# Gate products of a Griffin recurrent block: four float32 matmuls replaced by twelve float32r ones per pair of blocks, and moved half a weight tile to a tile and a half later

## The reference, cut to what matters

```python
u = jnp.einsum('bsd,de->bse', h, w_in) + b_in          # 1024 -> 2048
x_br = u[..., :D_RNN]
y_br = jax.nn.gelu(u[..., D_RNN:], approximate=True)
xp = jnp.pad(x_br, ((0, 0), (CONV_WIDTH - 1, 0), (0, 0)))
xc = conv_b + xp[:, 0:S] * conv_w[0]
for tap in range(1, CONV_WIDTH):
    xc = xc + xp[:, tap:tap + S] * conv_w[tap]
xb = xc.reshape(B, S, N_RG_BLOCKS, RG_BLOCK)             # 8 blocks of 128
r = jax.nn.sigmoid(jnp.einsum('bsnc,nce->bsne', xb, w_ga) + b_ga).reshape(B, S, D_RNN)
ig = jax.nn.sigmoid(jnp.einsum('bsnc,nce->bsne', xb, w_gx) + b_gx).reshape(B, S, D_RNN)
log_a = -RG_C * r * jax.nn.softplus(-a_param)
a = jnp.exp(log_a)
mult = jnp.sqrt(-jnp.expm1(2.0 * log_a))
b_seq = mult * (ig * xc)
# hs[t] = a[t] * hs[t-1] + b_seq[t]
out = hs * y_br
return jnp.einsum('bse,ed->bsd', out, w_o) + b_o
```

## Time and profile before

| what | value |
|---|---|
| median of 3 runs | 977.24 us (976.72 to 977.33) |
| span of the profiled execution | 975.9 us |
| what the runs have around that span | 1.3 us |
| PE busy | 968.3 us, 99% of the span |
| DVE, ACT, POOL busy | 70%, 60%, 7% |
| granted TensorE clock | full in all 40 slices |
| recurrent stage (`rin` 0 to `rout` 3) on PE | about 313.4 to 398.4 us |
| gate products (L589) | 16 matmuls in 32 records, 324.6 to 348 us |

### The profile page before, as it was taken

How to read it: one execution, slowest core, us unless ns; L and a number is a source line. 1 busy time by engine, 2 the same in 40 slices (tenths; PEclk the granted TensorE clock), 3 DMA queues, 4 the chain that set the end, 5 groups by cost and what they waited for, 6 DMA issues and landing times.

```text
span 975.9 us, 13399 instructions
## 1 busy us (share of the span) xinstructions
PE 968.3 (99%) x5146; PEld 826.0 (85%) x5146; DVE 680.5 (70%) x1161; ACT 588.6 (60%) x1042; POOL 66.2 (7%) x80
## 2 busy tenths in 40 slices
PE   8999999999999999999999999999999999999997
PEld 6887788888888898888888888888888888988886
DVE  5877786666568789666665588778767554877564
ACT  6777755454457897645454467547876555684443
POOL 1322110000000242000000000000011000000000
PEclk9999999999999999999999999999999999999999
DMA  9753545655455445555655556445543544335551
GB/s 368 296 194 134 184 173 186 224 176 211 174 196 185 146 165 192 182 187 184 226 178 207 177 198 250 173 175 188 198 165 105 193 148 170 132 133 209 177 189 44
DMA packets 27119, 180.33 MB, mean 185 GB/s; under 512 B 2992, under 2 KB 3888, under 8 KB 6320
## 3 DMA queue, kind: packets, MB, share of 16 engines
q1 hardware_dynamic: 26336, 176.98, 50.7%
q0 software_dynamic: 288, 2.10, 0.6%
q10 hardware_dynamic: 432, 0.39, 0.1%
HBM read 178.41 MB, written 1.05 MB: 184 GB/s over the span
## 4 chain that ended last, share of the span: by engine, by line
PE 99%; DMA 1%; DVE 0%; ACT 0%; SPq 0%; issue 0%; DVEq 0%
PE bank L338 25%; PE bank L293 16%; PE bank L295 16%; PE bank L294 16%; PE bank L346 13%; PE bank L308 1%; PE bank L468 1%; PE bank L484 1%; PE bank L589 1%; PE bank L518 1%; PE bank L309 1%; DMA front<-in_front 1%; PE bank L529 1%; PE bank L404 0%; PE bank L399 0%; PE bank L400 0%
## 5 line engine op out<-in xcount | busy, mean ns | idle before, releaser
L1349 DVE TENSOR_TENSOR lo<-raw,hi 128x1024 fp32r<-128x1024 f32 x318 | 375.9, 1229 | 20.1 <-ACT hi L822 19.9
L822 ACT ACTIVATE hi<-raw 128x1024 fp32r<-128x1024 f32 x318 | 320.3, 1050 | 100.1 <-PE bank L295 98.2
L338 PE MATMUL bank<-X,hi 128*128 128x512 f32 x1016 | 266.3, 394 | 0.0
L338 PEld LDWEIGHTS bank<-X,hi 128*128 128x128 f32 x1016 | 185.0, 189 | 32.8
L346 PEld LDWEIGHTS bank<-X,lo 128*128 128x128 f32 x1016 | 138.5, 190 | 10.1
L346 PE MATMUL bank<-X,lo 128*128 128x256 f32 x1016 | 141.6, 282 | 0.0
L853 ACT ACTIVATE bt<-bank 128x256 f32<-128x256 f32 x135 | 51.0, 380 | 141.5 <-PE bank L338 133.1
L1363 DVE TENSOR_TENSOR zr<-bank,bt 128x256 f32<-128x256 f32 x64 | 27.2, 424 | 108.9 <-ACT bt L853 108.9
L293 PE MATMUL bank<-hi,zh 128*128 128x512 f32 x256 | 100.0, 390 | 0.0
L295 PE MATMUL bank<-hi,zl 128*128 128x512 f32 x256 | 99.8, 390 | 0.0
L294 PE MATMUL bank<-lo,zh 128*128 128x512 f32 x256 | 99.6, 389 | 0.0
(11 more groups left out here) (345 smaller groups left out, 1420.5 us busy)
## 6 DMA issues: line engine op xcount, KB each, us to landing
raw<-in_w SPq DMA_DIRECT2D x64, 1024.0 KB, 4.7
raw<-in_rin SPq DMA_DIRECT2D x8, 1024.0 KB, 4.8
raw<-in_wk SPq DMA_DIRECT2D x4, 1024.0 KB, 10.3
raw<-in_wq SPq DMA_DIRECT2D x4, 1024.0 KB, 8.3
raw<-in_wo SPq DMA_DIRECT2D x4, 1024.0 KB, 4.7
raw<-in_mk SPq DMA_DIRECT2D x4, 1024.0 KB, 4.8
raw<-in_mv SPq DMA_DIRECT2D x4, 1024.0 KB, 4.8
raw<-in_rout SPq DMA_DIRECT2D x4, 1024.0 KB, 4.6
```

The costliest lines, as they stand in the source:

```text
L338: return PE.matmul(bank[b][:, :], wh[:, c:c + P], x[:, k_, :, :].rearrange("p a b -> p (a b)"), start=k_ == 0, stop=k_ == NC - 1, skip_gro ...
L822: ACTE.activation(hi[u_ % HIS][:, c], raw[u_ % RAW][:, c], ACT.Copy).then_inc(hi_cut, 1)
L1349: DVE.tensor_tensor(lo[u_ % RAW][:, c], raw[u_ % RAW][:, c], hi[u_ % HIS][:, c].bitcast(F32), ALU.subtract).then_inc(lo_cut, 1)
```

## The change

The gate weights `gw` and the convolution output `xc` are now split into float32r parts. ACT rounds `gw` into `gwh` and DVE subtracts to `gwl`, in two pieces each of 128x1024, inside the first MLP (steps 8 and 10). ACT rounds `xc` two blocks at a time into `xch` (`xc_highs`, 128x512), and DVE makes `xcl` (`xc_lows`). `xch` and `xcl` have room for four blocks. `gates(n)` on PE is now two `mm3`, six matmuls. The places move: blocks 0 and 1 stand in the middle of tile 2, blocks 2 and 3 in the middle of tile 3, blocks 4 and 5 in the first half of tile 4 and blocks 6 and 7 in the first half of tile 5 (each after its sixth of eight steps). On ACT every pair of gates is read one `to_x` later, and `xc_highs(i)` closes each step. The loads and their queues stay; POOL's load of `gw` goes to another slot.

```diff
-    gw = slot("gw", 14, [2, NC, P])
+    gw = slot("gw", 8, [2, NC, P])
+    gwh, gwl = slot("gwh", 14, [2, NC, P], F32R), slot("gwl", 4, [2, NC, P], F32R)
+    xch, xcl = slot("xch", 11, [4, S], F32R), slot("xcl", 11, [4, S], F32R, off=4096)
...
-                    if j == 1 and k_ == 4:
+                    if j == 0 and k_ == 6:
                         for n in within:
                             gates(n)
...
         def gates(n):
-            p.wait_ge(xc_made, n + 1)
-            p.wait_ge(gatew_in, 16)
+            p.wait_ge(xc_low, n // 2 + 1)
+            p.wait_ge(gw_low, 2)
             for m, b in ((0, 6 * (1 - n % 2)), (1, 7 - 6 * (n % 2))):
                 done = fill(("gate", n, m), b)
-                PE.matmul(bank[b][:, 0:S], gw[:, m, n, :], xc[:, n, :], start=True, stop=True).then_inc(done, 1)
+                mm3(bank[b][:, 0:S], gwh[:, m, n, :], gwl[:, m, n, :], xch[:, n % 4, :], xcl[:, n % 4, :], True, True).then_inc(done, 1)
...
         for i in range(1, 4):
-            cols("rin", i, X2, (2, 3) if i % 2 else (4, 5))
-            gates(2 * i - 2)
-            gates(2 * i - 1)
-        plain("rin", 4, X, (4, 5), (6, 7))
-        for i in range(5, 8):
+            half("rin", i, 0, X2, (4, 2)[i % 2])
+            if i > 1:
+                gates(2 * i - 4)
+                gates(2 * i - 3)
+            half("rin", i, 1, X2, (5, 3)[i % 2])
+        plain("rin", 4, X, (4, 5), (4, 5))
+        plain("rin", 5, X, (2, 3), (6, 7))
+        for i in range(6, 8):
             plain("rin", i, X, (2, 3) if i % 2 else (4, 5))
...
# ACT, in the first MLP; DVE has the matching subtraction into gwl
+                if n == 0 and i in (8, 10):
+                    m_ = i // 2 - 4
+                    a.wait_ge(gatew_in, 16)
+                    ACTE.activation(gwh[:, m_, :, :], gw[:, m_, :, :], ACT.Copy).then_inc(gw_high, 1)
...
# ACT
+        def xc_highs(i):
+            n = 2 * i
+            a.wait_ge(xc_made, n + 2)
+            if i >= 2:
+                a.wait_ge(*full["gate", n - 3, 1])
+                a.wait_ge(xc_low, i - 1)
+            ACTE.activation(xch[:, n % 4:n % 4 + 2, :], xc[:, n:n + 2, :], ACT.Copy).then_inc(xc_high, 1)
...
         for i in range(4):
             to_x(i)
-            if i:
-                gates(2 * i - 2)
-                gates(2 * i - 1)
+            if i > 1:
+                gates(2 * i - 4)
+                gates(2 * i - 3)
+            xc_highs(i)
         at_tile("rin", 4)
-        gates(6)
-        gates(7)
+        gates(4)
+        gates(5)
...
         to_y(4, ACT.Identity)
+        gates(6)
+        gates(7)
...
# DVE
+        def xc_lows(i):
+            n = 2 * i
+            d.wait_ge(xc_high, i + 1)
+            DVE.tensor_tensor(xcl[:, n % 4:n % 4 + 2, :], xc[:, n:n + 2, :], xch[:, n % 4:n % 4 + 2, :].bitcast(F32),
+                              ALU.subtract).then_inc(xc_low, 1)
...
         def to_x(i):
             lo_to(2 * (T_OF["rin", i] + 2))
+            if i:
+                xc_lows(i - 1)
...
         for i in range(4):
             to_x(i)
+        lo_to(2 * (T_OF["rin", 4] + 2) + 1)
+        xc_lows(3)
         lo_to(2 * (T_OF["rin", 4] + HIS))
```

More of the change, by code:

```diff
@@ L118, in build @@
     tap_made, xc_made, t_made = sem("tap_made"), sem("xc_made"), sem("t_made")
+    gw_high, gw_low, xc_high, xc_low = sem("gw_high"), sem("gw_low"), sem("xc_high"), sem("xc_low")
     gi_made, a_made, aa_made, mass_made, root_made, drive_made = (
@@ L1530, in mlp @@
                     at_tile(f"w2_{n}", i - 1)
+                if n == 0 and i in (8, 10):
+                    m_ = i // 2 - 4
+                    d.wait_ge(gw_high, m_ + 1)
+                    DVE.tensor_tensor(gwl[:, m_, :, :], gw[:, m_, :, :], gwh[:, m_, :, :].bitcast(F32), ALU.subtract).then_inc(gw_low, 1)
         mlp(0, 0, "wo")
```

## The result

The changed kernel takes 981.18 us (median of 5 runs, 980.51 to 981.95) against 977.33 us for the kernel before (976.72 to 977.85): a ratio of 1.0041, 95% interval 1.003 to 1.0051. It is slower by 3.85 us. The profiled span went from 975.9 to 979.2 us.

A forecast was written before the change was run, and what follows sets the result against it. It took PE to bound the kernel, busy 968.3 of 975.9 us. Waits 1.8 + 0.4 + 1.3 and restarts 0.4, less 1.15 saved, gave 2.7 us on 977.24: 979.9 us, range 977.3 to 981.7.

The forecast's parts named there:

- PE saves 1.15 us: Four gate places on PE: float32r products take 5.76 us where float32 ones took 6.9, saving 1.15 us.
- First place, 1.8 us: Gates of blocks 2 and 3: PE waits 1.4 us, then 0.4, for banks that ACT's sigmoids free; together 1.8 us.
- Second place, 0.4: Gates of blocks 4 and 5 in rin 4: bank 6 just in time, bank 0 late by 0.4 us.
- Third place, 1.2 to 1.3: Start of rin 7: PE waits 1.2 to 1.3 us for bank 2, freed by ACT's copy of group 10.
- Restart, 0.4: Matmuls behind each of four real PE stops: 0.1 us lost each, 0.4 in all, no loss of clock priced.
- What is late next: At rout 0: gl, 2.0 us ahead before, would be ready at 376.8 against PE at 379.3, so no wait.
- A: Recurrent stage: ACT reaches the gates in time, no waits, only PE's saving remains; 976.1 us, chance 0.12.
- B: At rin 7: group 10's copy comes in time, so only the gate banks cost; 978.5 us, chance 0.13.
- C: At rout 0: DVE loses 3 us more beside POOL's products, PE waits 1.5 us again; 981.4 us, chance 0.08.
- D: At blocks 2 and rin 7: ACT's table load holds it as long again, 1.3 us each; 982.5 us, chance 0.05.
- E: Gate products on PE: float32r cheaper than 0.12 or float32 dearer, saving 1.7 us; 979.3 us, chance 0.05.
- the 0.20 that the prediction counted to the gates: Seven L338 behind four float32 gate matmuls take 1.81 us, not 1.61; the extra 0.20 us was charged to the gates.

The follow-up runs named there:

- e1: Changed kernel with each gate product one float32 matmul of the rounded high parts, low parts left out of the product: 981.62 us, ratio 1.0044.
- e2: Changed kernel with ACT's table load for the sigmoids put ahead of the first rounding of xc: 980.65 us, ratio 1.0035.
- e5: Changed kernel with the gates of blocks 2 to 5 half a tile later on PE, ACT and DVE orders untouched: 980.82 us, ratio 1.0041.
- e3: Changed kernel with ACT's copies of groups 10 and 11 moved ahead of the second eight exponentials: 981.10 us, ratio 1.0043.
- e4: Kernel before with the gates moved to the new places, float32 products, no roundings or differences: 981.22 us, ratio 1.0041.
- e11: Kernel before with float32r parts and products for blocks 0 and 1 alone, at the old places: 976.93 us, ratio 0.9997.
- e9: Changed kernel with the edit of e3, and ACT's cut, DVE's first low half and first gl for rout 0 pulled ahead: 980.24 us, ratio 1.0037.
- e10: Changed kernel with the edits of e2, e3, e5 and e9 together: 979.30 us, ratio 1.0026.
- e8: Changed kernel with the gates back at the old places behind whole tiles, float32r parts kept: 981.20 us, ratio 1.0043.

## Why the prediction was right in direction and 1.3 us short

The forecast was 979.9 us, slower; measured 981.18, in the range.

- *PE saves 1.15 us.* Right: 1.44 us a place as said, 0.12 apart. e1 gives only 0.43 back, since the waits take up the rest.
- *First place, 1.8 us.* Right in place and releaser; 1.72 + 0.25 = 1.97. The table load ends at 335.00 where 335.4 less the 0.54 us by which this run's stage starts earlier gives 334.9. e2 shows that the load is what stands in front of the sigmoid.
- *Second place, 0.4.* Measured 0.12 + 0.25 = 0.37. The split was wrong (none and 0.4).
- *Third place, 1.2 to 1.3.* 1.45, released by ACT's copy to `yb`, as said.
- *Restart, 0.4.* 0.44 over these five stops, of which I had counted four. Full clock at each, as priced. In e5 a longer stop was not so.
- *What is late next.* This step failed, for 0.77 of the 1.1 us that the sum lacked (0.69 and a restart); the rest is in the terms above. What is left of the 1.3 us is the base, 977.33 in place of 977.24, and rounding. I took `gl` for the last thing that `rout` 0 waits for, ready at 374.67 and so 2.0 us ahead. But behind `gl` on DVE stands the low part of `rout` 0 itself, two halves of some 1.2 us. DVE in the kernel before, then in the changed one:

```profile
374.59 2.35 DVE L1349 TENSOR_TENSOR lo<-raw,hi 128x1024 fp32r<-128x1024 f32 x2
```

```profile
377.89 0.75 DVE L1639 TENSOR_TENSOR gl<-tt,gh 128x256 fp32r<-128x256 f32 x2
378.56 2.35 DVE L1370 TENSOR_TENSOR lo<-raw,hi 128x1024 fp32r<-128x1024 f32 x2
```

Before, the first half ended at about 375.8 and PE came at 376.65: the margin was 0.85 us and not 2.0. In the changed kernel `gl` ends at 378.64, 0.3 us before PE's last matmul of `mv` 1 starts (378.96) and so not late, and the first half of `lo` at 379.78; PE starts at 379.88. The view of waits has this stop under "issue". That the low part releases it is read from the times: in the changed kernel, e1, e2, e3, e4 and e11 PE's first matmul of `rout` 0 starts 0.10 us behind the end of this half, whatever the stop. It is borne out by e9: with this half pulled ahead the stop goes from `rout` 0, and the next is put down to `lo`. And DVE was later than I played it: its `gl` starts 4.0 us later than in the earlier trace rows in a stage that started 0.54 earlier, so it slipped by 4.5 where I had reckoned 2.1 (376.8 against 374.67). I had let idle time take up part of the slip, and there is none to take it up (see e10). It took both errors: with `lo` behind a `gl` at 376.8 its first half would have been there at 378.0, ahead of PE at 379.3, and with the true slip but `gl` the last thing there is no stop either.

Of the rivals, A and B fell. C had the right place, and its 981.4 us is nearer to the measured 981.18 than my forecast, but that is luck: it priced a stop of 1.5 us by `gl`, because DVE would lose more time under POOL's products. DVE loses no more there than before: from the first scan to the first `gl` it takes 9.66 us in the kernel before and 9.67 in the changed one. D fell for the place of the load: the sigmoid starts at 335.00, with the load ending at 334.99; there is no drain in the rows, as there was none before. E fell: the distance is 0.12.

What stays open: why the granted clock fell in e5, and how long the stages of these kernels are in other runs than the profiled one.

## What to carry to other kernels

- When PE is full, a cheaper matmul pays only if what feeds it costs nothing on engines that are full soon after. Here the rounding and the difference of one pair came out at `rout` 0, 50 us later (e11), by way of ScalarE, which is busy for all of 350 to 370. Look at the first stretch where a helper engine is busy for all of a window, and carry a delay through it whole. Count the margin behind it from the last thing in the helper's list that PE needs, not from the first.
- Move a product later and its readers move too. The wait for an input becomes a wait for a bank, and the chain of exponentials behind it starts later as a whole. An edit that removes one stop is worth only what the next stop on the path doesn't take: 1.43 us of stop gone gave 0.74 (e2), and 1.45 gave 0.01 (e3).

## What the runs showed of the hardware

- A stop of PE of 1.99 us (e5) was followed by 3.4 us at granted clock 0.50. In the profiles, stops of 1.56 us in the changed kernel, 1.61 in e3 and 1.75 in e8 were followed by full clock. By the mean clocks not every run of e5 had the slow stretch. No run looks between 1.75 and 1.99 us or asks why.
- Behind every stop the second matmul is 0.07 to 0.11 us late at full clock, where both are float32r.
- DVE takes longer beside POOL's products. In the kernel before, two scans took 1.80 us with them (from 371.54) and 1.26 without (377.53), two multiplications 1.83 (369.79) and 0.73 (373.27). These are rows of one trace; no run moves the products.
- A float32 matmul costs something behind its end as well: the second L341 behind float32 gates starts 0.42 us after the first (e1 at 329.29, e11 at 333.65), where 0.23 is usual. Behind float32r gates it does not: in e11 no such distance follows blocks 0 and 1. This is the 0.20 that the prediction counted to the gates.
